# The compressed keys of a block-sparse attention layer: token copies and block products moved into the projection of the queries

## The chip, the cores and the metric

One core of a Trainium2 chip. The time is device microseconds of one execution of the whole program; the program runs a stack of layers, and the change touches one stage of one of them.

## The reference, cut to what matters

The last mixer of the stack (the "odd" layer) projects 512 tokens of width 1024 to queries and to three pairs of keys and values, rotates queries and keys, and compresses one pair: 31 overlapping blocks of 32 tokens, each flattened with a position term added and sent through two small products with a gelu between.

```python
def compress(x, pe, w1, w2):
    B, T, G, d = x.shape
    chunks = x.reshape(B, T // CMP_STRIDE, CMP_STRIDE, G, d)
    blocks = jnp.concatenate([chunks[:, :-1], chunks[:, 1:]], axis=2) + pe[None, None, :, None, :]
    flat = blocks.transpose(0, 1, 3, 2, 4).reshape(B, -1, G, CMP_LEN * d)
    return jnp.einsum('bngf,fe->bnge', jax.nn.gelu(flat @ w1), w2)

def nsa_mixer(q, kc_raw, vc_raw, ks, vs, kw, vw, gates, pe, w1, w2, pos):
    ...
    k_cmp = compress(rope(kv(kc_raw), pos), pe[0], w1[0], w2[0])
    v_cmp = compress(kv(vc_raw), pe[1], w1[1], w2[1])
    ...
        s = jnp.einsum('bqghd,bngd->bqghn', qb, k_cmp).astype(jnp.float32) * scale
        p_cmp = safe_softmax(s, (cmp_end[None, :] <= t[:, None])[:, None, None, :])
```

Here T = 512, CMP_LEN = 32, CMP_STRIDE = 16, CMP_HIDDEN = 128, four groups of 64 dimensions.

## The kernel before, in words

Each engine has its own instruction stream; a stage is one block of five streams with waits on semaphores, and a barrier of all engines stands between two stages.

**The projection** (`project_rope`, on the machinery of `projection`) makes 16 tiles of 128 output columns by 512 tokens in 4 turns of 4 tiles. Tile n is tile b of turn i, n = 4i + b. A tile is 8 k-steps of three products (L136, L137, L138: high and low halves of weights and activations), 24 products of 512 columns, accumulated in PSUM bank b. SyncE (SP) loads the tile's 512 KB of weights into ring slot b, ScalarE (ACT, L120) makes the high half, GpSimd (POOL, L125) the low half, TensorE (PE) multiplies. A tile that is rotated ("turned") is then copied by ACT to `raw` (L905), multiplied by a 128 x 512 swap matrix on PE into bank 4 + b (L912), and put together by VectorE (DVE) in three instructions (L922, L923, L925). A plain tile needs one DVE instruction (L918). PE does the swap of tile n after the products of tile n + 1, at the end of a turn after its own. The loads of turn i + 1 wait, slot by slot, for POOL's low half of turn i (`hold` in `sync`).

The order of the tiles is 8 query tiles, then kc (2), ks (2), kw (2), vc (2): the last two are plain. At the head of this stage SP issues `load`: the compression's weights w1 (two of 1 MB, L3761), `pe_rows` (L3762), w2 (L3763) and two masks (L3764, L3765), seven DMAs on one semaphore `cmp_in`, and only then the weights of turn 1. Nothing in the stage waits for `cmp_in`. The first two tiles' weights were split in the stage ahead, so PE starts at once.

**The compression** (`compressed`) is the stage behind it. SP copies the kc and vc tiles into `tokens` (8 DMAs, L3791), once as they are and once shifted by one token; PE transposes the position rows (L3803) which ACT writes into `tokens` as a fifth group; PE makes 16 products for keys (z = 0) and 16 for values (z = 1) of 5 x 31 = 155 columns, whose 31 columns of a group lie 16 elements apart (L3810); ACT takes the bias and the gelu (L3846, L3849); PE multiplies by w2 (L3815, L3819) with a DVE copy between (L3869); ACT moves the results (L3852, L3854). PE then makes the block scores (L3827: 64 matmuls for 4 query tiles), DVE and ACT the softmax (L3875 to L3890), PE the transposes (L3833). ACT and POOL also split the first two tiles of the output weights here. An fp32 matmul shows in the trace as two records.

Of the kernel before, what the change touches and what calls it, by code (L numbers as in the profile page):

```python
# [523 lines left out]
def projection(c, ctx, w, evacuate, rhs=None, ahead=None, whole=None, before={}, after={}, norm=None, between={}, unrolled=(), alternate=False,  # L524
# [364 lines left out]
def project_rope(c, w, tables, scales, dest, ahead=None, before={}, after={}, beside=None, unturned=None, first=None):  # L889
# [3 lines left out]
    with c.stage() as ctx:  # L893
# [5 lines left out]
        turned = lambda i, b: unturned is None or i * per_turn + b < unturned  # L899

        def act(eng, i, wait_tile, bank_free, split):
            for b in range(per_turn):
                wait_tile(b)
                if turned(i, b):
                    nc.scalar.activation(raw[:, b, :], c.ps[:, b, :], ACT.Copy).then_inc(copied, 1)  # L905
                split(b)

        def pe(eng, i, b, bank_free):
            if not turned(i, b):
                return  # L910
            eng.wait_ge(copied, i * per_turn + (b + 1))
            nc.tensor.matmul(c.ps[:, 4 + b, :], table(i, b)[0][:, :], raw[:, b, :], start=True, stop=True).then_inc(swapped, 1)  # L912

        def dve(eng, i, wait_tile, bank_free):
            for b in range(per_turn):
                if not turned(i, b):
                    wait_tile(b)
                    nc.vector.tensor_tensor(dest(i, b), c.ps[:, b, :], c.rstd[:, :], ALU.mult).then_inc(bank_free, 1)  # L918
                    continue
                scale = scales(i, b) if callable(scales) else scales[b]  # L920
                eng.wait_ge(swapped, i * per_turn + (b + 1))
                nc.vector.scalar_tensor_tensor(dest(i, b), c.ps[:, b, :], scale, table(i, b)[1][:, :], ALU.mult, ALU.mult).then_inc(scaled, 1)  # L922
                nc.vector.scalar_tensor_tensor(part[:, b % 2, :], c.ps[:, 4 + b, :], scale, table(i, b)[2][:, :], ALU.mult, ALU.mult).then_inc(scaled, 1)  # L923
                eng.wait_ge(scaled, i * (2 * per_turn) + (2 * b + 2))
                nc.vector.tensor_tensor(dest(i, b), dest(i, b), part[:, b % 2, :], ALU.add).then_inc(bank_free, 1)  # L925
                if beside is not None:
                    beside(eng, i * per_turn + b)
        how = dict(ahead=ahead, before=before, after=after, unrolled=("all" if unturned is not None else () if beside is None else ("dve",)))
# [2747 lines left out]
def odd_weights(A):  # L3676
# [3 lines left out]
    KEYS = [OD[name] + b * P for name in ("kc", "ks", "kw", "vc") for b in range(2)]  # L3680

    def tile(i, j):
        if i < 2:
            return [((slice(None), slice(None), slice(64 * b, 64 * b + 64)),
                     view[:, :, i * 512 + (b * 256 + j * 64):i * 512 + (b * 256 + j * 64) + 64]) for b in range(2)]
        col = KEYS[(i - 2) * 4 + j]
# [11 lines left out]
def odd_mix(c, A, w, ahead):  # L3698
# [8 lines left out]
    with c.stage() as ctx:  # L3707
        oT = ctx.sbuf("oT", [P, KD, T])
        with c.stage() as mixing:
# [8 lines left out]
            def projections(load, vcT):  # L3718
                with c.stage() as inner:
                    w["rows"].buffers = dict(vs=vs, vw=vw, gates=gates)  # L3720
                    rope = RopeTables(c, inner, (64,))
                    with c.stage() as norming:
                        late = Late(c, norming, rows=True)
                        project_rows(c, w["rows"], {"sp": rope.load, "dve": lambda dve: rope.scale(dve, late)}, w["qkv"], late)
                    dests = [qT[:, n, :] for n in range(KD)] + [kT[:, n, :] for n in range(6)] + [vcT[:, n, :] for n in range(2)]
                    project_rope(c, w["qkv"], [rope.of[64]] * 4, lambda i, b: NSA_D ** -0.5 if i < 2 else 1.0, lambda i, b: dests[4 * i + b], w["out"],
                                 {"sp": load, "dve": lambda dve: reorder_gates(c, dve, gates, order)}, unturned=len(dests) - 2)
            compressed(c, A, w, qT, kT, order, pcT, vcr, projections)
# [16 lines left out]
def compressed(c, A, w, qT, kT, order, pcT, vcr, projections):  # L3745
# [5 lines left out]
    with c.stage() as ctx:  # L3751
# [6 lines left out]
        def load(sp):  # L3758
# [9 lines left out]
        projections(load, vcT)  # L3768
        w["out"].can_split = 2
        split_ahead = SplitAhead(c, w["out"], 2)  # L3770
        tokens = ctx.sbuf("tokens", [P, 2, 5, T])
        pe_bias = ctx.sbuf("pe_bias", [P, 2])
        hidden = ctx.sbuf("hidden", [P, 2, 2, 2, NP])
        spread = ctx.sbuf("spread", [P, 2, 2, 2, NP])
        kcT = ctx.sbuf("kcT", [P, 2, NP])
        s = ctx.sbuf("s", [P, TT, NSA_H, NP])
        stat = ctx.sbuf("stat", [P, 2, TT, NSA_H])
        padded, made, biased, hid, spread_done, kv_made, kv_done, pe_turned, pe_moved = (
            ctx.sem(n) for n in ("padded", "made", "biased", "hid", "spread_done", "kv_made", "kv_done", "pe_turned", "pe_moved"))
        scored, less, exped, weighed, turned, copied = (ctx.sem(n) for n in ("scored", "less", "exped", "weighed", "turned", "copied"))  # L3780
        tokens_in = [ctx.sem(f"tokens_in{z}") for z in range(2)]
        source = (kT, vcT)
        half = lambda b: slice(64 * b, 64 * b + 64)
        with nc.Block() as block:

            @block.sync
            def _(sp):
                for z in range(2):
                    for b in range(2):
                        for after in range(2):  # L3790
                            sp.dma_start(tokens[half(after), z, 2 * b:2 * b + 2, 0:T - after], source[z][half(b), 0:2, after:T]).then_inc(tokens_in[z], 16)  # L3791

            @block.gpsimd
            def _(pool):
                nc.gpsimd.memset(tokens[:, :, 4, :], 0.0).then_inc(padded, 1)
                nc.gpsimd.memset(hidden[:, :, :, :, :], 0.0).then_inc(padded, 1)
# [3 lines left out]
            def _(pe):  # L3800
                pe.wait_ge(cmp_in, n_in)
                for z in range(2):
                    tr = nc.tensor.transpose(c.ps[:, 1, z * PAIRS_L:(z + 1) * PAIRS_L], pe_rows[:, z, :], c.ident[0:PAIRS_L, 0:PAIRS_L])  # L3803
                tr.then_inc(pe_turned, 1)
                pe.wait_ge(pe_moved, 1)
                for z in range(2):
                    pe.wait_ge(tokens_in[z], 16 * 4)
                    for m in range(PAIRS_L):
                        block_tokens = tokens[:, z, :, 2 * m:2 * m + CMP_STRIDE * (CMP_N - 1) + 1:CMP_STRIDE]
                        mm = nc.tensor.matmul(c.ps[:, 4 + 2 * z, 0:5 * CMP_N].rearrange("p (g n) -> p g n", g=5), w1[:, z, m, :], block_tokens,  # L3810
                                              start=(m == 0), stop=(m == PAIRS_L - 1))
                    mm.then_inc(made, 1)
                pe.wait_ge(hid, 4)
                for b in range(2):
                    mm = nc.tensor.matmul(c.ps[half(b), 0, 0:2 * NP], w2[:, 0, :], hidden[:, 0, b, :, :].rearrange("p i n -> p (i n)"), start=True, stop=True)  # L3815
                mm.then_inc(kv_made, 1)
                pe.wait_ge(spread_done, 2)
                for i in range(2):
                    mm = nc.tensor.matmul(c.ps[:, 1, i * NSA_D:(i + 1) * NSA_D], spread[:, i, :, :, :].rearrange("p a b n -> p (a b n)"), w2[:, 1, :],  # L3819
                                          start=True, stop=True)  # L3820
                mm.then_inc(kv_made, 1)
                pe.wait_ge(kv_done, 2)
# [14 lines left out]
            def _(act):  # L3837
                act.wait_ge(pe_turned, 1)
                act.wait_ge(padded, 1)
                nc.scalar.activation(tokens[:, :, 4, 0:2 * PAIRS_L:2], c.ps[:, 1, 0:2 * PAIRS_L].rearrange("p (z m) -> p z m", z=2), ACT.Copy).then_inc(pe_moved, 1)  # L3840
                split_ahead.high(act)
                split_ahead.high(act)
                act.wait_ge(padded, 2)
                for z in range(2):
                    act.wait_ge(made, z + 1)
                    nc.scalar.activation(pe_bias[:, z:z + 1], c.ps[:, 4 + 2 * z, 4 * CMP_N:4 * CMP_N + 1], ACT.Copy).then_inc(biased, 1)  # L3846
                    act.wait_ge(biased, z + 1)
                    for b in range(2):
                        nc.scalar.activation(hidden[:, z, b, :, 0:CMP_N], c.ps[:, 4 + 2 * z, 2 * b * CMP_N:2 * (b + 1) * CMP_N].rearrange("p (i n) -> p i n", i=2),  # L3849
                                             ACT.Gelu_apprx_tanh, bias=pe_bias[:, z:z + 1]).then_inc(hid, 1)  # L3850
                act.wait_ge(kv_made, 1)
                nc.scalar.activation(kcT[:, :, :], c.ps[:, 0, 0:2 * NP].rearrange("p (i n) -> p i n", i=2), ACT.Copy).then_inc(kv_done, 1)  # L3852
                act.wait_ge(kv_made, 2)
                nc.scalar.activation(vcr[:, :, :], c.ps[:, 1, 0:P].rearrange("p (i d) -> p i d", i=2), ACT.Copy).then_inc(kv_done, 1)  # L3854
# [9 lines left out]
            def _(dve):  # L3864
                v = nc.vector
                step = Chain(dve, c.dve_step)
                dve.wait_ge(hid, 4)
                for a in range(2):
                    v.tensor_copy(spread[:, :, a, :, :], hidden[:, 1, :, :, :].rearrange("p b i n -> p i b n")).then_inc(spread_done, 1)  # L3869
# [114 lines left out]
```

## Time and profile before

| what | value |
|---|---|
| median of 3 runs | 3468.77 us (3464.75 to 3474.76) |
| the profiled execution, time | 3476.28 us |
| its span | 3474.3 us |
| mean granted clock of TensorE | 0.956 |
| stages of the change (projection and compression) | about 2723 to 2882 us of the span |

Busy shares are means over the whole span. A matmul's record has a modelled end, so the distance between starts is its price, not its duration. The granted clock is 1.0 at 2.4 GHz and 0.5 at 1.2 GHz.

### The profile page before, as it was taken

To read this page: it belongs to the slowest core of one execution; us is meant where nothing else is said; L and a number is where in the kernel's file an instruction comes from. 1 tells how busy PE (TensorE), PEld (TensorE's weight loads), DVE (VectorE), ACT (ScalarE), POOL (GpSimd) and SP (SyncE) were. 2 spreads that over 40 slices of the span, in tenths; PEclk is the share of its full clock that TensorE was granted. 3 is DMA by queue.
4 is the path that set the end of the run, shared out by engine and by line. 5 is a ranking of instruction groups with operands and counts; after the bars stand their busy time and mean duration, and the time that the engine had idled before them with its cause. 6 is when DMAs were issued, how large, how long until landed. Compare 5 with 4: busy or idle time off the path is not lost. (4 is left out here: it accounts for less than half of the span.)

```text
span 3474.3 us, 48152 instructions
## 1 busy us (share of the span) xinstructions
PE 3255.7 (94%) x16380; PEld 2680.5 (77%) x16380; DVE 1825.2 (53%) x3756; ACT 1302.8 (37%) x2179; POOL 1328.3 (38%) x830
## 2 busy tenths in 40 slices
PE   7999999889889999999999986899999988989999
PEld 6867787789888888888888853478887874568887
DVE  6404324887748777777777387332221326642211
ACT  4234433345543333333334333333322215633322
POOL 2323352278862222222221322434444325734443
PEclk9889999999999999999999997889999988999999
DMA  5321242245569999999996310023333420033332
GB/s 120 80 70 32 73 115 74 67 148 180 180 256 337 323 326 320 324 322 323 330 319 221 74 49 25 6 79 97 97 90 99 116 57 1 1 85 97 97 90 80
DMA packets 453880, 502.00 MB, mean 144 GB/s; under 512 B 77408, under 2 KB 398240, under 8 KB 435824
## 3 DMA queue, kind: packets, MB, share of 16 engines
q1 hardware_dynamic: 430448, 363.77, 34.3%
q0 software_dynamic: 18432, 134.23, 10.5%
q10 hardware_dynamic: 4864, 2.23, 0.3%
q8 instruction: 80, 1.31, 0.2%
q14 instruction: 56, 0.46, 0.0%
HBM read 458.06 MB, written 38.80 MB: 143 GB/s over the span
## 5 line engine op out<-in xcount | busy, mean ns | idle before, releaser
L125 POOL TENSOR_TENSOR w_low<-w_ring,w_high 128x1024 fp32r<-128x1024 f32 (+3 forms) x317 | 755.0, 2385 | 1143.2 <-ACT w_high L120 1115.6
L136 PE MATMUL ps<-h_low,w_high 128*128 128x512 f32 (+1 forms) x2432 | 918.8, 378 | 54.1 <-POOL w_low L125 28.5
L137 PE MATMUL ps<-h_high,w_high 128*128 128x512 f32 (+1 forms) x2432 | 900.7, 370 | 0.0
L138 PE MATMUL ps<-h_high,w_low 128*128 128x512 f32 (+1 forms) x2432 | 900.5, 370 | 0.0
L136 PEld LDWEIGHTS ps<-h_low,w_high 128*128 128x128 f32 x2432 | 464.1, 191 | 125.5 <-POOL w_low L125 31.4
L137 PEld LDWEIGHTS ps<-h_high,w_high 128*128 128x128 f32 x2432 | 464.2, 191 | 63.6 <-issue 6.3
L138 PEld LDWEIGHTS ps<-h_high,w_low 128*128 128x128 f32 x2432 | 463.2, 190 | 57.0
L120 ACT ACTIVATE w_high<-w_ring 128x1024 fp32r<-128x1024 f32 (+3 forms) x317 | 323.5, 1025 | 124.1 <-PE ps L138 120.0
L136 PE MATMUL ps<-v_low,top 128*128 128x512 f32 x768 | 300.1, 391 | 5.6 <-DVE v_low L125 5.6
L138 PE MATMUL ps<-v_high,top_at 128*128 128x512 f32 x768 | 301.2, 392 | 0.0
L137 PE MATMUL ps<-v_high,top 128*128 128x512 f32 x768 | 301.1, 392 | 0.0
L120 ACT ACTIVATE v_high<-w_ring 128x1024 fp32r<-128x1024 f32 x128 | 135.5, 1059 | 263.7 <-PE ps L138 259.6
L3125 POOL DMA_INDIRECT room<-in_peer_uv_dram,idx_now x62 | 89.0, 1436 | 363.2 <-DVE sums L3264 356.5
L1584 POOL TENSOR_SCALAR probs<-probs,stat 128x128 f32<-128x128 f32 (+3 forms) x153 | 158.9, 1050 | 163.8 <-DVE stat L1602 87.6
L136 PEld LDWEIGHTS ps<-v_low,top 128*128 128x128 f32 x768 | 144.9, 189 | 35.4 <-DVE v_low L125 6.8
L821 DVE TENSOR_TENSOR xT<-xT,ps 128x512 f32<-128x512 f32 (+1 forms) x40 | 27.5, 688 | 270.1 <-PE ps L138 270.1
L138 PEld LDWEIGHTS ps<-v_high,top_at 128*128 128x128 f32 x768 | 144.7, 188 | 30.4
L137 PEld LDWEIGHTS ps<-v_high,top 128*128 128x128 f32 x768 | 144.7, 188 | 28.6
L2845 POOL TENSOR_SCALAR firsts<-keys,slots 128x128 f32<-128x128 f32 x168 | 153.7, 930 | 18.5 <-ACT slots L2935 18.5
L125 DVE TENSOR_TENSOR v_low<-w_ring,v_high 128x1024 fp32r<-128x1024 f32 x128 | 156.0, 1219 | 0.0
L3125 POOL DMA_INDIRECT ring<-in_peer_uv_dram,idx_now x63 | 80.7, 1281 | 156.2 <-DVE sums L3264 130.4
L1565 ACT ACTIVATE probs<-ps,stat 128x512 f32<-128x512 f32 (+3 forms) x186 | 96.8, 525 | 112.7 <-DVE stat L1621 110.0
(538 smaller groups left out, 5487.5 us busy)
## 6 DMA issues: line engine op xcount, KB each, us to landing
w_ring<-in_peer_uv_dram SPq DMA_DIRECT2D x128, 512.0 KB, 5.6
u_raw<-in_peer_uT_dram SPq DMA_DIRECT2D x78, 512.0 KB, 6.0
w_ring<-in_peer_uT_dram SPq DMA_DIRECT2D x50, 512.0 KB, 3.7
gates<-peer_gates SPq DMA_DIRECT2D x31, 768.0 KB, 10.2
w_ring<-in_ffn_w_gate_dram SPq DMA_DIRECT2D x44, 512.0 KB, 3.7
w_ring<-in_ffn_w_up_dram SPq DMA_DIRECT2D x44, 512.0 KB, 3.6
w_ring<-in_w_in_dram SPq DMA_DIRECT2D x36, 512.0 KB, 3.8
w_ring<-in_ffn_w_down_dram SPq DMA_DIRECT2D x32, 448.0 KB, 3.7
```

The costliest lines, as they stand in the source:

```text
L120: return nc.scalar.activation(rounded(high), whole, ACT.Copy)
L125: return eng.tensor_tensor(rounded(low), whole, high, ALU.subtract)
L136: nc.tensor.matmul(out, rounded(w_high), rounded(x_low), start=start, stop=False, **more)
L137: nc.tensor.matmul(out, rounded(w_high), rounded(x_high), start=False, stop=False, **more)
L138: return nc.tensor.matmul(out, rounded(w_low), rounded(x_high), start=False, stop=stop, **more)
L821: nc.vector.tensor_tensor(d, d, c.ps[:, first_bank + b + (tiles * (i % 2) if alternate else 0), :], ALU.add).then_inc(bank_free, w.parts)
L1565: nc.scalar.activation(probs[s % p_bufs][:, a, 0:width[t]], c.ps[:, score_bank(s, a), 0:width[t]], ACT.Exp, bias=top[:, s % p_bufs, a:a + ...
L1584: nc.gpsimd.tensor_scalar(of, of, inverse[:, s % p_bufs, a:a + 1], None, ALU.mult).then_inc(normed_pool, 1)
L2845: mark = nc.gpsimd.tensor_scalar(firsts[:, k % (FIRSTS * QUAD), :], keys[:, :], slots[:, n % 2, 0, k:k + 1], slots[:, n % 2, 2, k:k + 1], ...
L3125: nc.gpsimd.indirect_dma_start(ring[slot], None, uv, bass.IndirectOffsetOnAxis(ap=index, axis=0)).then_inc(gathered[slot], 16)
```

## The change

The order of the tiles becomes kc, vc (turn 0, vc plain), 8 query tiles (turns 1 and 2), ks, kw (turn 3). When DVE has finished tiles 0 to 3 it raises `given`, and SP, behind the loads of turn 1, issues the 8 token copies (into `oT`, free at this time) before the loads of turn 2. PE runs the products behind the swaps of tiles 8 to 11, now 124 columns each, with the position term as 32 separate matmuls of one column; the gelu follows at tile 12, w2 at tiles 13 and 15. The swap banks become 4 and 5 only, with a wait for the tile two back. The transposes of the position rows, and with them PE's wait for all seven DMAs of `cmp_in`, stand at the head of PE's stream of the projection. The next stage begins with the block scores.

```diff
@@ projection, sync
                 w.load(c, sp, i, b)
+            if "sp_turn" in before:
+                before["sp_turn"](sp, i)
@@ project_rope
+        plain = () if also is None else also.plain
+        swap_bank = lambda b: 4 + (b % 2 if plain else b)
...
                 split(b)
+                if also is not None:
+                    also.act_tile(eng, i * per_turn + b)
         def pe(eng, i, b, bank_free):
+            if turned(i, b):
+                if plain and i * per_turn + b >= 2:
+                    eng.wait_ge(bank_free, i * per_turn + (per_turn + b - 1))
+                eng.wait_ge(copied, nth(i, b))
+                nc.tensor.matmul(c.ps[:, swap_bank(b), :], table(i, b)[0][:, :], raw[:, b, :], start=True, stop=True).then_inc(swapped, 1)
+            if also is not None:
+                also.pe_tile(eng, i * per_turn + b)
@@ odd_weights
-    KEYS = [OD[name] + b * P for name in ("kc", "ks", "kw", "vc") for b in range(2)]
+    KEYS = [OD[name] + b * P for name in ("kc", "vc", "ks", "kw") for b in range(2)]
@@ odd_mix
-                                 {"sp": load, "dve": lambda dve: reorder_gates(c, dve, gates, order)}, unturned=len(dests) - 2)
+                                 {"sp": load, "sp_turn": also.sp_turn, "pool": also.pool, "pe": also.pe_first, "act": also.act_first,
+                                  "dve": lambda dve: reorder_gates(c, dve, gates, order)}, {"act": also.act_last}, unturned=len(dests), also=also)
@@ new
+class CompressedKeys:
+    plain = (2, 3)
+    products_at, kept_at, keys_at, spread_at, values_at = (8, 9, 10, 11), 12, 13, 13, 15
+    def pool(self, pool):
+        self.c.nc.gpsimd.memset(self.hidden[:, :, :, :, :], 0.0).then_inc(self.padded, 1)
+    def sp_turn(self, sp, i):
+        if i != 1:
+            return
+        sp.wait_ge(self.given, 1)
+        for z in range(2):
+            for b in range(2):
+                for after in range(2):
+                    to = self.tokens[self.half(after), 4 * z + 2 * b:4 * z + 2 * b + 2, 0:T - after]
+                    sp.dma_start(to, self.source[z][self.half(b), 0:2, after:T]).then_inc(self.tokens_in[z], 16)
+    def pe_first(self, pe):
+        c, n = self.c, CMP_LEN // 2
+        pe.wait_ge(self.cmp_in, self.n_in)
+        for z in range(2):
+            tr = c.nc.tensor.transpose(c.ps[:, 7, 256 + z * n:256 + (z + 1) * n], self.pe_rows[:, z, :], c.ident[0:n, 0:n])
+        tr.then_inc(self.turned, 1)
+    def act_first(self, act):
+        act.wait_ge(self.turned, 1)
+        c.nc.scalar.activation(self.pe_cols[:, :, :], ...).then_inc(self.moved, 1)
+    def pe_tile(self, pe, n):
+        if n in self.products_at:
+            z, part = divmod(self.products_at.index(n), 2)
+            if part == 0:
+                pe.wait_ge(self.moved, 1)
+                for m in range(PAIRS_L):
+                    mm(c.ps[:, 6 + z, 4 * CMP_N:4 * CMP_N + 1], self.w1[:, z, m, :], self.pe_cols[:, z, m:m + 1], start=(m == 0), stop=(m == PAIRS_L - 1))
+                pe.wait_ge(self.tokens_in[z], 16 * 4)
+            for m in range(part * PAIRS_L // 2, (part + 1) * PAIRS_L // 2):
+                block_tokens = self.tokens[:, 4 * z:4 * z + 4, 2 * m:2 * m + CMP_STRIDE * (CMP_N - 1) + 1:CMP_STRIDE]
+                made = mm(c.ps[:, 6 + z, 0:4 * CMP_N].rearrange("p (g n) -> p g n", g=4), self.w1[:, z, m, :], block_tokens, start=(m == 0), stop=(m == PAIRS_L - 1))
+            if part == 1:
+                made.then_inc(self.made, 1)
+        if n == self.keys_at:
+            ...  # w2 for the keys behind wait(hid, 4)
+        if n == self.values_at:
+            ...  # w2 for the values behind wait(spread_done, 2)
+    def act_tile(self, act, n):
+        if n == self.kept_at:
+            ...  # bias, gelu of z = 0 and 1
+    def act_last(self, act):
+        ...  # the copies to kcT and vcr, behind the last tile
+    def dve_tile(self, dve, n, bank_free):
+        if n == 3:
+            dve.wait_ge(bank_free, 8)
+            dve.sem_inc(self.given, 1)
+        if n == self.spread_at:
+            ...  # the two copies to spread
@@ compressed: the same steps, the zeroing of the fifth group and PE's wait for kv_done leave the stage
```

## Rows read from the trace of the kernel before

**Rows 1.** Part 1 of the page: busy time, share, instructions.

```profile
PE 3255.7 (94%) x16380; PEld 2680.5 (77%) x16380; DVE 1825.2 (53%) x3756; ACT 1302.8 (37%) x2179; POOL 1328.3 (38%) x830
```

**Rows 2.** Windows: start:end, length, busy per engine, PEclk, DMA share, GB/s.

```profile
2775.00:2800.00 25.00, 25.00 (x103) 19.09 (x103) 12.53 (x12) 6.18 (x8) 9.16 (x5) 1.00 0.31 85
2825.00:2852.00 27.00, 18.52 (x74) 14.79 (x74) 0.36 (x2) 5.23 (x12) 5.84 (x4) 0.81 0.33 79
2852.00:2868.00 16.00, 13.35 (x128) 13.22 (x128) 8.88 (x17) 3.49 (x6) 0.00 (x0) 0.52 0.00 1
```

**Rows 3.** Timeline of PE around the compression: start, length, instruction, idle before.

```profile
2822.93 0.39 PE L138 MATMUL ps<-h_high,w_low 128*128 128x512 f32 x1
2825.70 0.36 PE L3803 MATMUL ps<-ident,pe_rows 16*128 16x16 f32 x2 [2.38 <-PEq L205]
2832.67 17.16 PE L3810 MATMUL ps<-tokens,w 128*128 128x155 f32 x64 [6.61 <-DMA tokens<-kT]
2850.65 0.34 PE L3815 MATMUL ps<-hidden,w 128*64 128x64 f32 x4 [0.81 <-ACT hidden L3849]
2852.07 13.35 PE L3827 MATMUL ps<-kcT,qT 64*128 64x32 f32 x128 [0.37 <-ACT vcr L3854]
```

**Rows 4.** Timeline of PE in the projection: its first product, tiles, swaps.

```profile
2723.20 0.47 PE L136 MATMUL ps<-h_low,w_high 128*128 128x512 f32 x1 [2.00 <-PEq L618]
...
2740.55 1.02 PE L912 MATMUL ps<-raw,swap 128*128 128x512 f32 x2
...
2746.90 1.97 PE L912 MATMUL ps<-raw,swap 128*128 128x512 f32 x4
```

**Rows 5.** Timeline of SP: the loads ahead of turn 1, the token copies.

```profile
2729.58 0.43 SPq L3765 DMA_DIRECT2D masks<-in_c_cmp_seen_dram  x1
...
2825.65 3.10 SPq L3791 DMA_DIRECT2D tokens<-kT  x4
2828.80 4.00 SPq L3791 DMA_DIRECT2D tokens<-vcT  x4
```

**Rows 6.** DMA issues by line: count, KB each, us from issue to landing.

```profile
w_ring<-in_od_w_in_dram SPq DMA_DIRECT2D x24, 256.0 KB, 3.2
...
tokens<-vcT SPq DMA_DIRECT2D x2, 256.0 KB, 4.8
...
masks<-in_c_cmp_seen_dram SPq DMA_DIRECT2D x1, 64.0 KB, 2.8
```

**Rows 7.** Windows of 1 us, block products L3810 alone: PE, PEld, PEclk.

```profile
2833.00:2834.00 1.00, 1.00 (x5) 1.00 (x5) 0.50 1.12 270
...
2835.00:2836.00 1.00, 1.00 (x6) 0.94 (x5) 0.70 0.74 172
...
2838.00:2839.00 1.00, 1.00 (x5) 0.77 (x5) 1.00 0.00 0
```

**Rows 8.** L2177, small fp32 matmuls: its group (ns min/median/max), 1 us windows.

```profile
L2177 PE MATMUL ps<-c_re,reach x64: 259/259/373, 82.9 to 91.4; 64*128 64x16 f32 x64
...
85.00:86.00 1.00, 1.00 (x22) 1.00 0.00 0
...
89.00:90.00 1.00, 1.00 (x14) 0.50 0.00 0
```

**Rows 9.** Windows of 1 us, all PE work, where the granted clock falls.

```profile
2825.00:2826.00 1.00, 0.30 (x2) 0.68 0.00 0
...
2852.00:2853.00 1.00, 0.93 (x14) 0.84 0.00 0
```

**Rows 10.** Timeline of DVE: rotations, the last tile.

```profile
2747.95 0.69 DVE L922 SCALAR_TENSOR_TENSOR qT<-ps,cos 128x512 f32<-128x512 f32 x1 [2.64 <-PE ps L912]
...
2811.52 0.69 DVE L922 SCALAR_TENSOR_TENSOR kT<-ps,cos 128x512 f32<-128x512 f32 x1 [7.09 <-PE ps L912]
...
2812.84 0.69 DVE L925 TENSOR_TENSOR kT<-kT,part 128x512 f32<-128x512 f32 x1
...
2823.35 0.69 DVE L918 TENSOR_TENSOR vcT<-ps,rstd 128x512 f32<-128x512 f32 x1 [2.87 <-PE ps L138]
```

More of the change, by code:

```diff
@@ L886, in project_swiglu, with project_rope @@
                       after={"dve": lambda eng: eng.wait_ge(dest_low, 2 * w.turns + 2)}), ready
-def project_rope(c, w, tables, scales, dest, ahead=None, before={}, after={}, beside=None, unturned=None, first=None):
+def project_rope(c, w, tables, scales, dest, ahead=None, before={}, after={}, beside=None, unturned=None, first=None, also=None):
     nc = c.nc
@@ L898, in project_rope @@
         table = tables if callable(tables) else lambda i, b: tables[b]
-        turned = lambda i, b: unturned is None or i * per_turn + b < unturned
+        plain = () if also is None else also.plain
+        turned = lambda i, b: i * per_turn + b not in plain if plain else unturned is None or i * per_turn + b < unturned
+        nth = lambda i, b: i * per_turn + (b + 1) - (sum(x <= i * per_turn + b for x in plain) if plain else 0)
+        swap_bank = lambda b: 4 + (b % 2 if plain else b)
         def act(eng, i, wait_tile, bank_free, split):
@@ L918, in dve @@
                     nc.vector.tensor_tensor(dest(i, b), c.ps[:, b, :], c.rstd[:, :], ALU.mult).then_inc(bank_free, 1)
+                    if also is not None:
+                        also.dve_tile(eng, i * per_turn + b, bank_free)
                     continue
                 scale = scales(i, b) if callable(scales) else scales[b]
-                eng.wait_ge(swapped, i * per_turn + (b + 1))
+                eng.wait_ge(swapped, nth(i, b))
                 nc.vector.scalar_tensor_tensor(dest(i, b), c.ps[:, b, :], scale, table(i, b)[1][:, :], ALU.mult, ALU.mult).then_inc(scaled, 1)
-                nc.vector.scalar_tensor_tensor(part[:, b % 2, :], c.ps[:, 4 + b, :], scale, table(i, b)[2][:, :], ALU.mult, ALU.mult).then_inc(scaled, 1)
-                eng.wait_ge(scaled, i * (2 * per_turn) + (2 * b + 2))
+                nc.vector.scalar_tensor_tensor(part[:, b % 2, :], c.ps[:, swap_bank(b), :], scale, table(i, b)[2][:, :], ALU.mult, ALU.mult).then_inc(scaled, 1)
+                eng.wait_ge(scaled, 2 * nth(i, b) if plain else i * (2 * per_turn) + (2 * b + 2))
                 nc.vector.tensor_tensor(dest(i, b), dest(i, b), part[:, b % 2, :], ALU.add).then_inc(bank_free, 1)
@@ L927, in dve @@
                     beside(eng, i * per_turn + b)
+                if also is not None:
+                    also.dve_tile(eng, i * per_turn + b, bank_free)
         how = dict(ahead=ahead, before=before, after=after, unrolled=("all" if unturned is not None else () if beside is None else ("dve",)))
@@ L3716, in odd_mix, with projections @@
             vcr = mixing.sbuf("vcr", [P, 2, NSA_D])
-            def projections(load, vcT):
+            def projections(load, vcT, also):
                 with c.stage() as inner:
@@ L3742, in reorder_gates, with __init__ @@
     step.wait()
-def compressed(c, A, w, qT, kT, order, pcT, vcr, projections):
+class CompressedKeys:
+    plain = (2, 3)
+    products_at, kept_at, keys_at, spread_at, values_at = (8, 9, 10, 11), 12, 13, 13, 15
+    def __init__(self, c, ctx, cmp_in, n_in, w1, w2, pe_rows, source, tokens, kcT, vcr, room):
+        self.c, self.cmp_in, self.n_in, self.w1, self.w2, self.pe_rows, self.source, self.tokens, self.kcT, self.vcr = (
+            c, cmp_in, n_in, w1, w2, pe_rows, source, tokens, kcT, vcr)
+        NP = CMP_N + 1
+        self.pe_cols = room[:, 2, 0:CMP_LEN].rearrange("p (z m) -> p z m", z=2)
+        self.pe_bias = room[:, 3, 0:2]
+        self.hidden, self.spread = (room[:, k, 0:8 * NP].rearrange("p (z b i n) -> p z b i n", z=2, b=2, i=2) for k in range(2))
+        self.padded, self.turned, self.moved, self.given, self.made, self.biased, self.hid, self.spread_done, self.kv_made, self.kv_done = (
+            ctx.sem(n) for n in ("padded", "pe_turned", "pe_moved", "keys_given", "made", "biased", "hid", "spread_done", "kv_made", "kv_done"))
+        self.tokens_in = [ctx.sem(f"tokens_in{z}") for z in range(2)]
+        self.half = lambda b: slice(64 * b, 64 * b + 64)
+    def pool(self, pool):
[16 more added lines that the diff above has]
+    def act_first(self, act):
+        c, n = self.c, CMP_LEN // 2
+        act.wait_ge(self.turned, 1)
+        c.nc.scalar.activation(self.pe_cols[:, :, :], c.ps[:, 7, 256:256 + 2 * n].rearrange("p (z m) -> p z m", z=2), ACT.Copy).then_inc(self.moved, 1)
+    def pe_tile(self, pe, n):
+        c, mm, PAIRS_L = self.c, self.c.nc.tensor.matmul, CMP_LEN // 2
+        if n in self.products_at:
[11 more added lines that the diff above has]
+        if n == self.keys_at:
+            pe.wait_ge(self.hid, 4)
+            for b in range(2):
+                made = mm(c.ps[self.half(b), 6, 0:2 * (CMP_N + 1)], self.w2[:, 0, :], self.hidden[:, 0, b, :, :].rearrange("p i n -> p (i n)"), start=True, stop=True)
+            made.then_inc(self.kv_made, 1)
+        if n == self.values_at:
+            pe.wait_ge(self.spread_done, 2)
+            for i in range(2):
+                made = mm(c.ps[:, 7, i * NSA_D:(i + 1) * NSA_D], self.spread[:, i, :, :, :].rearrange("p a b n -> p (a b n)"), self.w2[:, 1, :], start=True, stop=True)
+            made.then_inc(self.kv_made, 1)
+    def act_tile(self, act, n):
+        c, copy = self.c, self.c.nc.scalar.activation
+        if n == self.kept_at:
+            act.wait_ge(self.padded, 1)
+            for z in range(2):
+                act.wait_ge(self.made, z + 1)
+                copy(self.pe_bias[:, z:z + 1], c.ps[:, 6 + z, 4 * CMP_N:4 * CMP_N + 1], ACT.Copy).then_inc(self.biased, 1)
+                act.wait_ge(self.biased, z + 1)
+                for b in range(2):
+                    copy(self.hidden[:, z, b, :, 0:CMP_N], c.ps[:, 6 + z, 2 * b * CMP_N:2 * (b + 1) * CMP_N].rearrange("p (i n) -> p i n", i=2),
+                         ACT.Gelu_apprx_tanh, bias=self.pe_bias[:, z:z + 1]).then_inc(self.hid, 1)
+    def act_last(self, act):
+        c, copy = self.c, self.c.nc.scalar.activation
+        act.wait_ge(self.kv_made, 1)
+        copy(self.kcT[:, :, :], c.ps[:, 6, 0:2 * (CMP_N + 1)].rearrange("p (i n) -> p i n", i=2), ACT.Copy).then_inc(self.kv_done, 1)
+        act.wait_ge(self.kv_made, 2)
+        copy(self.vcr[:, :, :], c.ps[:, 7, 0:P].rearrange("p (i d) -> p i d", i=2), ACT.Copy).then_inc(self.kv_done, 1)
+        act.wait_ge(self.kv_done, 2)
+    def dve_tile(self, dve, n, bank_free):
[3 more added lines that the diff above has]
+        if n == self.spread_at:
+            dve.wait_ge(self.hid, 4)
+            for a in range(2):
+                self.c.nc.vector.tensor_copy(self.spread[:, :, a, :, :], self.hidden[:, 1, :, :, :].rearrange("p b i n -> p i b n")).then_inc(self.spread_done, 1)
@@ L3748, in compressed @@
+def compressed(c, A, w, qT, kT, order, pcT, vcr, projections, tokens):
     nc = c.nc
@@ L3767, in compressed @@
         vcT = ctx.sbuf("vcT", [P, 2, T])
-        projections(load, vcT)
+        kcT = pcT[:, 3, P:P + 2 * NP].rearrange("p (i n) -> p i n", i=2)
+        projections(load, vcT, CompressedKeys(c, ctx, cmp_in, n_in, w1, w2, pe_rows, (kT, vcT), tokens, kcT, vcr, pcT))
         w["out"].can_split = 2
         split_ahead = SplitAhead(c, w["out"], 2)
[L3771 to L3775, printed above, removed]
         s = ctx.sbuf("s", [P, TT, NSA_H, NP])
         stat = ctx.sbuf("stat", [P, 2, TT, NSA_H])
-        padded, made, biased, hid, spread_done, kv_made, kv_done, pe_turned, pe_moved = (
-            ctx.sem(n) for n in ("padded", "made", "biased", "hid", "spread_done", "kv_made", "kv_done", "pe_turned", "pe_moved"))
         scored, less, exped, weighed, turned, copied = (ctx.sem(n) for n in ("scored", "less", "exped", "weighed", "turned", "copied"))
-        tokens_in = [ctx.sem(f"tokens_in{z}") for z in range(2)]
-        source = (kT, vcT)
         half = lambda b: slice(64 * b, 64 * b + 64)
         with nc.Block() as block:
[L3786 to L3791, printed above, removed]
             @block.gpsimd
             def _(pool):
-                nc.gpsimd.memset(tokens[:, :, 4, :], 0.0).then_inc(padded, 1)
-                nc.gpsimd.memset(hidden[:, :, :, :, :], 0.0).then_inc(padded, 1)
                 split_ahead.low(pool)
@@ L3800, in _ @@
             def _(pe):
[L3801 to L3822, printed above, removed]
                 for t in range(TT):
```

34 lines of the change are left out of this document (6 added, 28 removed).

## Prediction

> **What bounds the kernel now.** I read the page first: TensorE is busy for 94% of the span [rows 1], so the question in any stage is what PE does and what it waits for. The windows by stage come next. Inside the projection PE is busy 25.00 of 25.00 us at granted clock 1.00 while DVE, ACT and POOL have half of their time or more free; between 2825 and 2852 PE is busy 18.5 of 27 us, and between 2852 and 2868 it does the block scores at clock 0.52 [rows 2]. So the projection is bound by PE's work alone: whatever is put on PE there is paid in full. The timeline of PE then says what the 28.75 us between the last product of the projection (2822.93 + 0.39 = 2823.32) and the first block score (2852.07) consist of [rows 3]: a stage change (DVE's last tile ends at 2824.04 [rows 10], PE's next instruction is at 2825.70, so 1.66 us), a wait for the token copies until 2832.67, 17.16 us of block products, and a short chain of gelu, w2 and copies. The timeline of SP and the DMA issues show what the copies cost and, at the head of the projection, when the seven loads of `cmp_in` are home [rows 5, 6]. Windows of 1 us give the price of one small matmul at either clock [rows 7, 8] and where the clock changes [rows 7, 9]. The timeline of DVE gives the tail of a rotated tile [rows 10].
>
> **The gap that goes.** After the change the last tile is rotated. From the last product of all (call it E): the two swaps of tiles 14 and 15 start on PE, and DVE begins tile 14 1.05 us later, as at 2746.90 and 2747.95 [rows 4, 10]. One tile takes DVE 2.01 us when POOL is quiet (2811.52 to 2812.84 + 0.69 [rows 10]), which it is in the last turn, so DVE ends at E + 5.1. The w2 products of the values (4 records like the 0.34 us for 4 at 2850.65 [rows 3]) lie beside DVE. ACT's two copies stand behind DVE's end: I take 0.6 us (the interval from the w2 products at 2850.65 to the first score at 2852.07, 1.4 us, holds them and more [rows 3]). With the stage change of 1.66 us the first score comes at E + 7.35, where it was at E + 28.75: 21.4 us less. E itself has two swaps fewer ahead of it; a further swap in a row takes 1.97 - 1.02 = 0.95 us [rows 4], so 1.9 us more. Together **-23.3 us**.
>
> **What PE gets inside the projection.** Nothing covers these, since PE has no idle time there.
> - 32 block products, 64 records. Before, 64 of 155 columns take 17.16 us, 0.268 each, and the count of records in a microsecond is the same at clock 0.50 as at 1.00 [rows 3, 7]: the product is not bound by the array's clock. A swap reads its 512 columns in a row and takes 0.95 us for two records [rows 4], 0.93 ns a column, where the block product takes 1.73 ns: about half of its price comes with the operand whose elements lie 16 apart. If all of it goes by columns, 124 of them cost 0.215 us: 13.7 us. That is my value, since the swap's part and the stride's are both paid for a column read. Bounds: 0.268 unchanged, 17.2 us; the swap's price of 0.115, 7.4 us.
> - 32 matmuls of one column, 64 records that load 128 columns of weights each. The nearest row has 16 columns: 22 records touch one microsecond at clock 1.00, each 0.26 long, so one starts every 1.26 / 22 = 0.057 us; at clock 0.50, 14 touch it, about 0.1 us each [rows 8]. 3.6 us, at most 6.7. In the old form the position term cost 31 of 155 columns.
> - w2 for the keys, 0.3 us [rows 3].
>
> Sum **+17.6 us** (11.3 to 24.2). So moving the products alone saves 23.3 - 17.6 = 5.7 us: PE pays for almost all that it no longer waits for.
>
> The SBUF page of the Trainium skill (SBUF — State Buffer, Door 1: The DMA port swizzle) says that an access pattern which crosses to a new 16-byte line at each element pays a penalty. By it the doubled price stays in the new place, 13.7 us; had the doubling come from something else in the old stage, the products would cost 7.4 us.
>
> **The wait that comes.** `pe_first` puts `wait_ge(cmp_in, 112)` ahead of PE's first product. SP issues the seven loads from the head of this same stage; the last starts at 2729.58 and lands 2.8 us later, 2732.4 [rows 5, 6]. Before, PE started at 2723.20 [rows 4] and nothing there waited for them. With the two transposes (0.36 us [rows 3]) the first product moves to 2732.75: **+9.55 us**. Nothing hides it, for all of the projection queues behind it on PE. ACT too waits for the transposes, with tile 3's split behind, but that is needed four tiles later.
>
> The idle also costs clock. Around the last stage change PE stopped at 2823.3 and the granted clock fell within 2825 to 2826 [rows 9]; it restarted at 2832.67 and the clock was back in the window 2835 to 2836, some 3 us later [rows 7]. Here PE would be idle for 11.5 us, restart at 1.2 GHz, and do half the work for 3 to 6 us: 1.5 to 3 us, I take **+2.0**.
>
> The Trainium skill (TensorE: Matmul & The Clock Gate, Part 1) says that the throttled clock is the default and activity releases it. By it the stall costs more than its length, about 11.5 us for 9.55; without it the sum would be 2 us lower.
>
> **At no cost, with the work that hides it.** (a) SP now stops for `given` behind the loads of turn 1, and the loads of turn 2 queue behind it. Tile 3 is ready at 2732.75 + 2.0 + 4 x 5.4 + 2 x 0.95 + 0.7 = 2759 (a tile's 24 products are 2746.90 - 2740.55 - 0.95 = 5.4 us [rows 4]); the 8 issues take 7.15 us [rows 5], the copies are home at about 2770 (4.8 us behind the last issue [rows 6]), and tile 8's weights, two issues and 3.2 us more, at about 2772. PE wants tile 8 at 2732.75 + 2.0 + 8 x 5.4 + 6 x 0.95 = 2783.7, and ACT (6.2 us for four tiles) and POOL (9.2) need about 4 us ahead of it for the halves [rows 2]: about 8 us of cover; without it each microsecond late is a microsecond of stall, with ACT's `raw` copies queued behind the late split. (b) The tokens are home 20 us before tile 8's swap. (c) The swap's new wait for the tile two back: DVE is busy 12.5 us for four tiles, 3.1 each [rows 2], and has more than a tile's 5.4 us. (d) Gelu with its table load and DVE's `spread` copies lie in turn 3, where both engines are over half free [rows 2]. (e) ACT's and POOL's splits of the output weights, which lay in the token wait, now lie beside the first block scores: per query tile PE gives the scores every 3.3 us, ACT is busy 0.9 and DVE 2.2 [rows 2]; should POOL's 5 us hold DVE's first tile up by 2 us, the 1.1 us that it has to spare in each later one give that back.
>
> **The block scores.** PE idles some 4.7 us before them, so they start at 1.2 GHz instead of spending 0.6 us at 2.4 GHz [rows 9]: **+0.3 us**. They were at 0.5 for the other 12.8 us anyhow.
>
> **Sum.** -23.3 + 17.6 + 9.55 + 2.0 + 0.3 = **+6.2 us**. The profiled execution took 3476.3 us (span 3474.3), the median of the runs is 3468.8, 7.5 us under it; I carry the difference over: 3468.8 + 6.2 = **3475.0 us**, 0.18% slower, inside the 0.3% (10.4 us) about which a measurement of this kernel can tell from no change.
>
> **Rivals.**
> - *Slower by more than 0.3%: the short matmuls bring the clock down.* Bursts of 16- and 32-column matmuls lost the full clock while PE never paused: L2177 went from 1.00 to 0.50 in its course [rows 8], the block scores ran at 0.50 throughout [rows 2]. Here 32 records of one column stand ahead of each half of the products, twice. If the clock falls in both: +3.0 us for those records and 2 us of products at half clock after each, +7 in all: 3482 us. It decides once both bursts do it. Against it: the old products ran up to and held 1.00 [rows 7], and a burst lasts 1.9 us. 0.15. Tile 8's weights would lead to the same side if they were over 12 us later than I have them, 0.03; the upper bound of the products alone, 3478.5, would not.
> - *A little faster: the stall is not there.* If PE's wait were satisfied at the head of the stage, 9.55 and 2.0 fall away: 3463 us. For it only that the loads are issued early; against it, their landing 9 us after PE's old start. 0.10.
> - *Faster by more than 0.3%*: the swap's price for the products (-6.3) with a full clock in the block scores. PE needs 128 x 0.057 = 7.3 us there instead of 13.35, DVE 2.2 us a tile becomes the bound, some -4.9: alone 3470, both 3464; only with the stall gone too is it 3452. 0.04.
> - *The change does nothing for PE*, since its work is only moved: that is the case forecast, with the token wait bought and the `cmp_in` wait paid.
>
> **How the numbers follow.** The forecast with its bounds (-6.3 for the products or +3.5, up to +1 for the clock) has 0.68, and lies at 3468 to 3480. The range takes in the clock rival above and the missing stall below, with the scatter of a median: 3462 to 3484. Slower: 0.15 + 0.03 and a small part of the forecast, 0.21; faster 0.04 and a little scatter, 0.06; the same 0.73.
>
> **What would show it.** First product of the projection at about 9.5 us behind where the stage starts it now, its idle put down to a load of `cmp_in`, and PEclk under 1 for its first microseconds. Block products at 0.21 us a record, single-column ones at 0.057. No idle of PE ahead of tile 8. First block score 6 us later than 2852 on the same scale. I am wrong if PE starts at once, if a window in turn 2 or 3 shows clock 0.5, or if PE waits for `w_low` in turn 2.

## The result, and the profile after

The changed kernel takes 3485.1 us (median of 12 runs, 3473.1 to 3490.7) against 3473.0 us of the kernel before in runs beside it (3464.0 to 3482.6): ratio 1.0034, 95% interval 1.0022 to 1.0045, so 12 us slower, clear of noise. I forecast 3475.0 with a range of 3462 to 3484 and most of the chance on "the same": the direction of the sum was right, its size half of what came, and the time lies 1.1 us outside the range. Part of that is not the change: I had built on 3468.8 us for the kernel before, and beside the changed kernel it ran at 3473.0. So 4.2 us of the 10.1 us between forecast and measurement come with the base, and 5.9 us are my error on the change. The ratios are of fast runs; one execution of the variant without one-column matmuls took 11841 us and is in none of them.

The page still shows PE at 94%, with 64 matmul records more:

```profile
PE 3263.1 (94%) x16444; PEld 2692.0 (77%) x16444; DVE 1820.9 (52%) x3756; ACT 1303.6 (37%) x2179; POOL 1331.4 (38%) x829
```

An execution of this program can be several microseconds early or late before it even reaches the stage (the profiled executions told of here reach it between 2707 and 2722 us). So I also measure inside the trace, from the last product of the stage ahead to the first of the bf16 matmuls (L131) that open the attention stage behind. The two ends, in the timeline of PE, for the kernel before:

```profile
2720.91 0.28 PE L138 MATMUL ps<-w_rows_high,h_low 128*128 128x256 f32 x1
...
2882.24 1.01 PE L131 MATMUL ps<-mask_causal,mask_ident 128*128 128x512 bf16 x2 [1.55 <-PEq L205]
```

That is 161.3 us. (PEq is PE's sequencer.) For the changed kernel, the same view with what lies between (L3798 transposes the position rows, L3813 is the one-column matmul, L3817 the block product, L920 the swap, L3904 the block scores):

```profile
2720.85 0.28 PE L138 MATMUL ps<-w_rows_high,h_low 128*128 128x256 f32 x1
2732.23 0.39 PE L3798 MATMUL ps<-ident,pe_rows 16*128 16x16 f32 x2 [11.09 <-DMA masks<-in_c_cmp_seen_dram]
2732.55 0.80 PE L136 MATMUL ps<-h_low,w_high 128*128 128x512 f32 x1
...
2795.11 4.59 PE L3813 MATMUL ps<-pcT,w 128*128 128x1 f32 x32
2799.57 3.75 PE L3817 MATMUL ps<-oT,w 128*128 128x124 f32 x16
...
2802.98 0.77 PE L136 MATMUL ps<-h_low,w_high 128*128 128x512 f32 x1
...
2819.75 3.63 PE L3813 MATMUL ps<-pcT,w 128*128 128x1 f32 x32
2823.24 3.63 PE L3817 MATMUL ps<-oT,w 128*128 128x124 f32 x16
2826.68 1.82 PE L920 MATMUL ps<-raw,swap 128*128 128x512 f32 x2
...
2855.76 2.04 PE L920 MATMUL ps<-raw,swap 128*128 128x512 f32 x4
2857.63 0.55 PE L3828 MATMUL ps<-w,pcT 128*128 128x64 f32 x4
2862.75 0.64 PE L3904 MATMUL ps<-pcT,qT 64*128 64x32 f32 x4 [4.57 <-PEq L205]
...
2893.43 1.01 PE L131 MATMUL ps<-mask_causal,mask_ident 128*128 128x512 bf16 x2 [1.55 <-PEq L205]
```

172.6 us: the 11.3 us more inside this stretch account for the 12 us, within the interval. PE is idle for 11.1 us until the last of the seven loads is home (2.0 us of that is the stage change, which the kernel before has too [rows 4]) and starts its products at 2732.55 instead of 2723.20 [rows 4]; the first block score comes at 2862.75 instead of 2852.07 [rows 3].

The other thing to see is the two bursts of L3813: from start to the next line's start 2799.57 - 2795.11 = 4.46 us and 2823.24 - 2819.75 = 3.49 us, where I had 1.8 us for each. The windows of the same stretch show the granted clock (third number from the right) under 1 around them, and PE busy throughout:

```profile
2795.00:2805.00 10.00, 10.00 (x55) 0.66 0.32 91
2805.00:2820.00 15.00, 15.00 (x67) 1.00 0.12 36
2820.00:2825.00 5.00, 5.00 (x40) 0.99 0.04 12
2825.00:2830.00 5.00, 5.00 (x19) 0.67 0.33 93
```

### The profile page after: what moved, and what is told of

Read it like the earlier page. It is cut to its first block and busy times, and to the rows that moved or that the text cites. A ratio compares the mean times of both kernels' runs of the same rounds, so it can differ in the third digit from the quotient of the medians.

```text
span 3485.9 us, 48290 instructions
## 1 busy us (share of the span) xinstructions
PE 3263.1 (94%) x16444; PEld 2692.0 (77%) x16444; DVE 1820.9 (52%) x3756; ACT 1303.6 (37%) x2179; POOL 1331.4 (38%) x829
## 3 DMA queue, kind: packets, MB, share of 16 engines
q0 software_dynamic: 18432, 134.23, 10.5%
## 5 line engine op out<-in xcount | busy, mean ns | idle before, releaser
L120 ACT ACTIVATE w_high<-w_ring 128x1024 fp32r<-128x1024 f32 (+3 forms) x317 | 323.9, 1026 | 137.4 <-PE ps L138 130.1
L120 ACT ACTIVATE v_high<-w_ring 128x1024 fp32r<-128x1024 f32 x128 | 135.6, 1060 | 265.2 <-PE ps L138 259.6
```

The lines of the kernel that those rows point to most:

```text
L120: return nc.scalar.activation(rounded(high), whole, ACT.Copy)
```

## The experiments

Where a stage length is given, it is the stretch just described (before 161.3, changed 172.6 us). Ratios are against the kernel before, run beside each. Two variants leave something out, and say so. Each stage length is read from one profiled execution, so the smallest differences, under 1 us, should not be leaned on.

**The wait at the head, added alone.** The kernel before, with one wait:

```diff
-        projections(load, vcT)
+        projections(load, vcT, lambda pe: pe.wait_ge(cmp_in, n_in))
...
-                                 {"sp": load, "dve": ...}, unturned=len(dests) - 2)
+                                 {"sp": load, "pe": wait, "dve": ...}, unturned=len(dests) - 2)
```

> The kernel before with one instruction more: PE waits for the seven loads ahead of the projection's first product. Nothing else is changed. Theory: first product 9.3 us later and 1.7 us of low clock, so 11 us slower than the kernel before (ratio 1.0032), nearly the whole loss of the change. Rival (the later stages absorb part of it, since the kernel before has waits for tokens and weights behind the projection): 5 us or less.

Ratio 1.0036 (1.0021 to 1.0051); stage 172.8 us, 11.4 more. One wait costs as much as the whole change. PE's timeline:

```profile
2718.05 0.28 PE L138 MATMUL ps<-w_rows_high,h_low 128*128 128x256 f32 x1
...
2729.35 0.80 PE L136 MATMUL ps<-h_low,w_high 128*128 128x512 f32 x1 [11.02 <-DMA masks<-in_c_cmp_seen_dram]
```

The first product stands 11.30 us behind the last of the stage ahead instead of 2.29, so 9.0 us of wait; from there to the last product PE needs 101.6 us instead of 99.7, 1.9 us more (the clock is at 0.50 for its first 4 us, as PE comes out of the pause), and the stretch from the first block score on is 0.5 us longer. No later wait absorbs any of it.

**The wait at the head, taken away from the change.**

```diff
-  "pool": also.pool, "pe": also.pe_first, "act": also.act_first,
+  "pool": also.pool,
...
+        if n == 5:
+            self.pe_first(pe)    # in pe_tile
...
+        if n == 6:
+            self.act_first(act)  # in act_tile
```

> The changed kernel with the wait for the seven loads, the two transposes and the copy of their result taken from the head of the projection and put behind tile 5's swap (PE) and tile 6's copy (ACT), where the loads have long landed. Theory (the wait at the head costs its 9.35 us and about 1.8 us of low clock after it): PE starts at about 2723.2 of the span at clock 1.00, 11.1 us faster than the changed kernel, so within 2 us of the kernel before. Rival (the wait is partly given back, because the tiles behind it then wait for weights that SP sends only after the token copies): 4 to 7 us faster only, with an idle of PE ahead of tile 8.

Ratio 1.0014 (1.0001 to 1.0027); stage 162.8 us, 9.8 less than the changed kernel and 1.5 more than the one before. PE starts 2.28 us behind the stage ahead and nowhere waits for weights: the rival, weights late behind the token copies, is out.

```profile
2713.56 0.28 PE L138 MATMUL ps<-w_rows_high,h_low 128*128 128x256 f32 x1
2715.84 0.47 PE L136 MATMUL ps<-h_low,w_high 128*128 128x512 f32 x1 [2.00 <-PEq L620]
```

The gain is 1.3 us under the theory's 11.1, though the pause and its low clock are gone. The clock still falls twice in turn 2, and the second fall lasts 6.8 us where it lasted 3.4 us in the changed kernel. So the 3.9 us at low clock that the head no longer has come back nearly whole (13.6 us at low clock in the projection, 14.1 in the changed kernel); why the second fall lasts longer here is open. The two falls by windows:

```profile
2777.00:2790.00 13.00, 13.00 (x68) 0.74 0.26 72
2790.00:2801.00 11.00, 11.00 (x50) 1.00 0.16 48
2801.00:2812.00 11.00, 11.00 (x57) 0.69 0.17 48
```

**Without the one-column matmuls** (the position term's product is left out):

```diff
-                for m in range(PAIRS_L):
-                    mm(c.ps[:, 6 + z, 4 * CMP_N:4 * CMP_N + 1], self.w1[:, z, m, :], self.pe_cols[:, z, m:m + 1], start=(m == 0), stop=(m == PAIRS_L - 1))
...
-                copy(self.pe_bias[:, z:z + 1], c.ps[:, 6 + z, 4 * CMP_N:4 * CMP_N + 1], ACT.Copy).then_inc(self.biased, 1)
+                copy(self.pe_bias[:, z:z + 1], c.ps[:, 6 + z, 0:1], ACT.Copy).then_inc(self.biased, 1)
```

> The changed kernel without the 32 matmuls of one column: the position term's product is left out (the column read for it is a product's). Theory (a matmul of one column behind a load of 128 x 128 weights costs 0.109 us a record, and the bursts of them bring the granted clock down): 7.0 us of records and 2 to 3 us of clock, so 9 to 10 us faster than the changed kernel, and clock 1.00 from tile 1 to tile 15. Rival (the clock falls for the strided products, not for the one-column ones): 7 us faster, with the clock still down once or twice in turns 2 and 3. Rival (0.057 us a record as predicted): 3.6 us.

Ratio 1.0010 (0.9996 to 1.0024); stage 163.1 us, 9.5 less than the changed kernel. The products in the same places with the same stride leave the clock alone:

```profile
2796.00:2806.00 10.00, 10.00 (x44) 1.00 0.37 103
2806.00:2824.00 18.00, 18.00 (x79) 1.00 0.21 59
2824.00:2850.00 26.00, 26.00 (x111) 1.00 0.07 21
```

So it is the one-column matmuls that bring it down, not the strided products: 7.0 us for 64 records at 0.109 us, and 2.5 us of clock. The kernel of the experiment before this one shows the same from the other side. Its bursts start at 2777.15 and 2801.79, the block products behind them at 2781.02 and 2806.32, and both times the clock falls while the burst is still running:

```profile
2779.00:2780.00 1.00, 1.00 (x11) 1.00 0.00 0
2780.00:2781.00 1.00, 1.00 (x7) 0.62 0.00 0
2803.00:2804.00 1.00, 1.00 (x11) 1.00 0.00 0
2804.00:2805.00 1.00, 1.00 (x7) 0.57 0.00 0
```

**The same matmuls over half of the rows** (64 rows of weights each, upper and lower in turn; the second half's sum is left out):

```diff
                 for m in range(PAIRS_L):
-                    mm(...)
+                    for two in range(2):
+                        mm(..., self.w1[self.half(two), z, m, :], self.pe_cols[self.half(two), z, m:m + 1], ...)
```

> The changed kernel with each one-column matmul cut into two over 64 rows of weights each, upper and lower half in turn, as in the rows the forecast took its price from; the second half's sum is left out of the bias. 128 records instead of 64. Theory (two records on different halves of the rows overlap, so the price of such a record is half of that of a full one): 0.055 us from start to start at full clock, the two bursts together 7 to 8 us as before. Rival (each record costs 0.109 us whatever its rows): bursts of 14 us together.

One execution, for the price alone. The two bursts of 64 records each:

```profile
2790.64 3.83 PE L3814 MATMUL ps<-pcT,w 64*128 64x1 f32 x64
2794.40 0.58 PE L3819 MATMUL ps<-oT,w 128*128 128x124 f32 x1
...
2814.11 3.74 PE L3814 MATMUL ps<-pcT,w 64*128 64x1 f32 x64
2817.77 0.46 PE L3819 MATMUL ps<-oT,w 128*128 128x124 f32 x1
```

3.76 and 3.66 us for 64: 0.058 us a record, half of the 0.109 of a record over all 128 rows. That is the price that I had read off L2177 [rows 8], whose weights are 64 rows too, upper and lower in turn. Each such pair costs as much as one record over all rows. Whether that is because two records on different halves overlap, or because half of the rows costs half, this variant can't tell, since it only has the two halves in turn.

**The one-column matmuls in four lots.** No wait at the head, and 8 of them behind each of tiles 4 to 7:

```diff
+        if 4 <= n <= 7:
+            for z in range(2):
+                for m in range(4 * n - 16, 4 * n - 12):
+                    mm(c.ps[:, 6 + z, 4 * CMP_N:4 * CMP_N + 1], self.w1[:, z, m, :], self.pe_cols[:, z, m:m + 1], ...)
...
-                for m in range(PAIRS_L):
-                    mm(...)
```

> The changed kernel without the wait at the head (transposes at tile 3) and with the one-column matmuls in four lots of 8 (16 records, 1.75 us) behind tiles 4 to 7 instead of two bursts of 16 (32 records, 3.5 us) ahead of the products. Theory (a burst of them brings the clock down): clock 1.00 throughout, 64 records at 0.109 us, the stage 2 to 3 us shorter than without the wait alone. Rival (it is their number and not the burst): the clock falls as often.

Stage 159.4 us in one execution, 3.4 less than with the two bursts. Each lot takes 1.70 us, 0.106 a record, and the clock stays:

```profile
2750.00:2772.00 22.00, 22.00 (x123) 1.00 0.62 145
2772.00:2836.00 64.00, 64.00 (x275) 1.00 0.18 49
```

The records cost the same, and in lots they cost no clock. The lots also lie a turn earlier, with no block products behind them; that the place matters is not ruled out by this run, but the falls inside the bursts, shown above, speak for the burst itself.

**The order of the tiles alone**, with the compression in its own stage as before:

```diff
+class PlainTiles:
+    plain = (2, 3)
...
-    KEYS = [OD[name] + b * P for name in ("kc", "ks", "kw", "vc") for b in range(2)]
+    KEYS = [OD[name] + b * P for name in ("kc", "vc", "ks", "kw") for b in range(2)]
```

> The new order of tiles and the two swap banks alone; the compression stays in its own stage as before. Theory (the last tile is now a rotated one, so that DVE ends later behind the last product): 3 to 3.5 us slower than the kernel before (6 us from the last product to the next stage instead of 2.4, minus the two swaps that then lie in that tail: +1.9 on PE before, so the first instruction of the next stage 4.3 us after the swaps' start against 2.4). Rival (the swap banks' new wait makes PE idle too): over 5 us slower, with idle of PE ahead of L920.

Ratio 1.0002 (0.9989 to 1.0014), which can't tell 2.5 us from none; stage 163.8 us, 2.45 more, somewhat under my 3 to 3.5. The tail is the longer one of a rotated tile, and PE waits ahead of no swap, so the new wait of the swap banks costs nothing.

**The position term on DVE, no wait at the head.** DVE sums w1 times the position column, and PE makes one product with a column of ones for each of keys and values:

```diff
+    sum_parts, sums_at = (5, 6, 8, 9), (9, 11)
...
+            if m == 0:
+                v.tensor_scalar(out, w, row, None, ALU.mult).then_inc(self.summed, 1)
+            else:
+                dve.wait_ge(self.summed, CMP_LEN // 2 * z + m)
+                v.scalar_tensor_tensor(out, w, row, out, ALU.mult, ALU.add).then_inc(self.summed, 1)
...
+            mm(c.ps[:, 6 + z, 4 * CMP_N:4 * CMP_N + 1], self.sums[:, z, :], c.ones[:, 0:1], start=True, stop=True).then_inc(self.bias_made, 1)
```

> The changed kernel without the wait at the head (transposes at tile 3) and with the position term summed on DVE: w1 times its position column, 16 instructions of 128 columns for each of keys and values, beside tiles 5, 6, 8 and 9, and on PE one product with a column of ones for each. Theory (the three costs are the wait, the one-column records and the clock that they cost, and moving the products was by itself a gain): the stage is 9.5 us shorter than without the wait alone, so 8 us shorter than the kernel before, ratio about 0.9975, clock 1.00 in the whole projection. Rival (the strided products inside the projection cost PE or its partners more than in their own stage): no faster than the kernel before. Rival (DVE's 32 small instructions with a wait each, 6 to 10 us, hold up the rotations): PE idle ahead of a swap.

Stage 152.9 us, 8.5 less than the kernel before. Ratio 0.9989 (0.9972 to 1.0005): the interval holds both that and no change, so by whole runs alone it would be unproven. The clock is 1.00 in the whole projection and DVE's 32 instructions (0.35 us each) hold up no swap:

```profile
2714.00:2764.00 50.00, 49.80 (x207) 1.00 0.78 193
2764.00:2829.00 65.00, 65.00 (x281) 1.00 0.18 49
```

**And PE kept at work ahead of the scores.**

```diff
             made.then_inc(self.kv_made, 1)
+            spin(c, 0, 14)
```

> As the one with the sums on DVE, and 14 bf16 matmuls of 512 columns without use on PE behind the last product of the projection, in the 3 us in which PE waits for DVE and ACT. Theory (the block scores run at low clock because of the pause ahead of them): the scores start at clock 1.00, DVE sets their pace, the stage is 3 to 5 us shorter. Rival (the short matmuls of the scores lose the clock by themselves, as the one-column ones do): the clock falls within a few us of their start and the gain is under 1.5 us.

Ratio 0.9973 (0.9957 to 0.9988), 3458.5 us against 3467.1: faster than the kernel before, clear of noise, and so than the changed one. Stage 151.1 us, 1.8 less than without the 14 matmuls. The scores start at full clock and lose it some 2 us later (they start at 2828.95, and PE is idle for only 1.55 us ahead of them, where it was 4.57):

```profile
2824.00:2829.00 5.00, 3.45 (x20) 1.00 0.00 0
2829.00:2834.00 5.00, 5.00 (x66) 0.70 0.02 3
2834.00:2846.00 12.00, 6.99 (x66) 0.50 0.00 0
```

So the theory had the start right and the gain wrong (3 to 5 us); the rival that the clock falls by itself is nearer.

## Why the prediction was right or wrong

The stages of the kernels make a ledger: 161.3 before; + 2.45 order alone; - 10.9 for moving the products with the position term on DVE (163.8 to 152.9); + 10.2 for the wait and its clock (152.9 to 163.1, the kernel without one-column matmuls); + 9.5 for the one-column matmuls (163.1 to 172.6). Each step is a difference of two single executions, and the 10.2 has about 0.3 us hidden in it that the kernel with the sums on DVE pays for its two products with ones.

- **The gap that goes**, -23.3. Right: from the last product's start to the first score 29.14 us before, 7.22 after, and two swaps (1.9) in that tail instead of ahead of it: -23.8.
- **Block products**, +13.7. Right: the four groups take 3.41, 3.20, 3.44 and 3.20 us, 13.3 in all, 0.20 a record at clock 1.00, as if the stride's part stayed; no run has the same products over contiguous columns, so what the price comes from is not shown. The price of the swap's contiguous columns, my lower bound, is out.
- **One-column matmuls**, +3.6, at most 6.7. **This is the step that failed.** They took 7.95 us, over the upper bound. I took the price of a record over 64 rows, upper and lower half in turn, for one over 128 rows; `64*128` stood in the row [rows 8]. The right price at clock 1.00 is twice that, 7.0 us; the rest is clock. The bound was wrong for the same reason: its row at clock 0.50 was of 64 rows too (and its 0.1 us gives 6.4 us, not 6.7).
- **The clock in turn 2**, a rival at 0.15 that I priced at +7 together with its records. It came, and it was the sign that I had named for being wrong: the clock fell around both bursts in the changed kernel and in the one without the wait. Its price was smaller, 2.5 us with what it added to the bursts (9.5 - 7.0). I had held against it that the bursts would last 1.9 us; they lasted 3.5 us because their price was wrong, and in lots of 1.7 us the clock in fact stays. So the wrong price very likely fed both terms, though no run has a burst of 32 records that lasts 1.9 us.
- **The wait**, +9.55 and +2.0 of clock. Right: 9.35 in the changed kernel, 9.0 + 1.9 alone. PE's idle names the mask's load, as I said it would.
- **What was to cost nothing.** Right. PE waits nowhere in turns 1 to 3. ACT did wait for tile 8's weights, as I had them (home at about 2772), ahead of its L120:

```profile
2771.52 1.06 ACT L120 ACTIVATE w_high<-w_ring 128x1024 fp32r<-128x1024 f32 x1 [1.94 <-DMA w_ring<-in_od_w_in_dram]
```

- **The scores**, +0.3: 0.5.

With 7.95 in place of 3.6 the sum is 10.5 us. The low clock behind the bursts adds 1.5 us (9.5 - 7.95), the other terms came about 1 us lower together (the gap 0.5, the products 0.4, the wait 0.2), and that makes some 11 of the 11.3 us of the stage. The range had its upper end from a fall of the clock with the wrong price of a record, not from both at once.

## What to carry to other kernels

Moving work off a gap into a stage where PE is always busy gains only the waits that went with it and what the new form no longer computes. Here that was 10.9 us: PE's idle time around the compression went from 12.5 us (order alone) to 4.6 us, and most of the rest is the 31 columns of the position term that left each block product. A single wait put at the head of such a stage can cost all of it, so wait for a load where its result is first used, not where the setup is written. A position term or bias as one-column products is dear: a record of one column cost 0.109 us here where one of 124 columns cost 0.20. Put it on an idle engine. When a price is read off a row of another shape, the rows of the array that it fills belong to the shape.

## What the runs showed of the hardware

- An fp32 record with one column over 128 rows of weights starts every 0.109 us at clock 1.00; over 64 rows, upper and lower half in turn, every 0.058 us.
- During or just behind a burst of 32 one-column records over 128 rows (3.5 us at full clock) the granted clock fell to 1.2 GHz, without a pause of PE: both times in the changed kernel, for 6.8 and 3.4 us, and both times in the one without the wait. The bursts of 64 records over 64 rows (3.7 us) did the same, twice. Four lots of 16 records over 128 rows (1.7 us each) were not followed by a fall. The block scores, 32 columns over 64 rows, lost a full clock 2 us after their start with PE idle for only 1.55 us ahead of them.
- The block product of 124 columns 16 elements apart took 0.20 us a record at clock 1.00 and about 0.21 at 0.50 (3.20 and 3.41 us for 16).
- The same stages ahead took 2707 to 2722 us in the profiled executions, so a few us are better read inside the trace than off whole runs.
